# Working the second pair of weight units low part first in the conv stage of a two-layer diffusion trunk

## What is computed

```python
def dwconv3(x, w):
    xp = jnp.pad(x, ((0, 0), (1, 1), (0, 0)))
    return xp[:, :-2] * w[0] + xp[:, 1:-1] * w[1] + xp[:, 2:] * w[2]

def short_conv_mixer(h, w_in, conv_w, w_out):
    y = h @ w_in                      # (256 x 2048) @ (2048 x 6144)
    gb, gc, xv = jnp.split(y, 3, axis=-1)
    return (gb * dwconv3(gc * xv, conv_w)) @ w_out
...
xl = xl + g1 * yl
```

## Time and profile before

| | |
|---|---|
| median of 3 runs | 2545.12 us (2542.32 to 2546.88) |
| the profiled execution | 2542.89 us |
| its span in the trace | 2541.2 us |
| PE, VectorE, ScalarE, GpSimd busy | 98%, 81%, 50%, 8% of the span |
| mean granted TensorE clock | 0.996 |
| input projection, S2 to S23 | 1452 to 1701 us of the span |
| output projection, O0 to O7 | 1701 to 1792 us of the span |

### The profile page before, as it was taken

One profiled execution on the slowest core, in us unless ns is written; L12 is line 12 of the kernel. 1 busy time (PEld: TensorE's weight loads), 2 busy tenths in 40 slices (PEclk: granted clock), 3 DMA queues, 4 the chain that ended last, 5 costly groups with the idle time before them and its releaser, 6 DMA issues.

```text
span 2541.2 us, 38436 instructions
## 1 busy us (share of the span) xinstructions
PE 2499.0 (98%) x13946; PEld 2158.5 (85%) x13946; DVE 2052.4 (81%) x2708; ACT 1265.4 (50%) x1712; POOL 198.6 (8%) x302
## 2 busy tenths in 40 slices
PE   6999999999999999999999999999999999999998
PEld 4778888777988888888888988888988888888886
DVE  6888987897898889987888799989988876764554
ACT  5422334686565555554444544445655555554443
POOL 1002221000000001100111011101000000000000
PEclk9999999999999999999999999999999999999999
DMA  9768987554778778987999699968688756666554
GB/s 355 270 220 267 302 280 232 165 181 148 249 235 270 263 242 277 291 253 235 297 289 299 232 314 349 322 221 276 228 277 270 258 177 196 186 188 203 192 193 147
DMA packets 442817, 625.65 MB, mean 246 GB/s; under 512 B 18693, under 2 KB 359063, under 8 KB 435505
## 3 DMA queue, kind: packets, MB, share of 16 engines
q1 hardware_dynamic: 401888, 450.94, 53.8%
q0 software_dynamic: 40464, 172.59, 21.1%
q10 hardware_dynamic: 320, 0.13, 0.0%
HBM read 621.50 MB, written 2.10 MB: 245 GB/s over the span
## 4 chain that ended last, share of the span: by engine, by line
PE 90%; DVE 5%; DMA 3%; ACT 2%; issue 1%; SPq 0%; DVEq 0%; ACTq 0%
PE ps L2014 46%; PE ps L2022 24%; PE ps L2359 6%; PE ps L2366 3%; PE ps L1934 2%; PE ps L1935 2%; PE ps L1936 2%; DMA raw<-in_sconv_w_in_dram 2%; DVE w_lo L1172 1%; PE ps L2138 1%; PE ps L2156 1%; DVE start_sum L1166 1%; PE ps L2091 1%; PE ps L2090 1%; PE ps L2092 1%
## 5 line engine op out<-in xcount | busy, mean ns | idle before, releaser
L642 ACT ACTIVATE w_hi<-raw 128x1024 fp32r<-128x1024 f32 (+1 forms) x792 | 822.3, 1048 | 913.4 <-PE ps L2022 406.5
L1172 DVE TENSOR_TENSOR w_lo<-raw,w_hi 128x1024 fp32r<-128x1024 f32 (+1 forms) x792 | 954.7, 1210 | 360.6 <-ACT w_hi L642 357.7
L2014 PE MATMUL ps<-xs,w_hi 128*128 128x512 f32 x3200 | 762.3, 393 | 0.5 <-DVE v_rows L1220 0.5
L2014 PEld LDWEIGHTS ps<-xs,w_hi 128*128 128x128 f32 x3200 | 592.2, 188 | 125.3 <-issue 6.7
L2022 PEld LDWEIGHTS ps<-xs,w_lo 128*128 128x128 f32 x3200 | 403.5, 191 | 12.7 <-issue 1.0
L2022 PE MATMUL ps<-xs,w_lo 128*128 128x256 f32 x3200 | 410.0, 283 | 0.7 <-DVE w_lo L1172 0.7
L2359 PE MATMUL ps<-w_hi,act 128*128 128x512 f32 x704 | 175.2, 390 | 0.0
L2014 PE MATMUL ps<-xs_sin,w_hi 128*128 128x512 f32 x704 | 170.0, 392 | 0.4 <-ACT w_hi L642 0.4
L2014 PE MATMUL ps<-act,w_hi 128*128 128x512 f32 x704 | 165.1, 390 | 0.0
L2359 PEld LDWEIGHTS ps<-w_hi,act 128*128 128x128 f32 x704 | 131.6, 188 | 27.1
L540 POOL DMA_DIRECT2D ada_ring<-in_w_ada_dram x128 | 91.0, 711 | 790.8 <-DVE ada_sum L1243 537.2
(11 more groups left out here) (269 smaller groups left out, 2976.3 us busy)
## 6 DMA issues: line engine op xcount, KB each, us to landing
raw<-in_ffn_w_up_dram SPq DMA_DIRECT2D x352, 512.0 KB, 4.7
ada_ring<-in_w_ada_dram POOLq DMA_DIRECT2D x176, 512.0 KB, 5.3
raw<-in_ffn_w_down_dram SPq DMA_DIRECT2D x152, 512.0 KB, 3.7
raw<-in_attn_w_qkv_dram SPq DMA_DIRECT2D x96, 512.0 KB, 4.9
broad_ring<-in_w_ada_dram POOLq DMA_DIRECT2D x48, 1024.0 KB, 6.1
raw<-in_sconv_w_in_dram SPq DMA_DIRECT2D x96, 512.0 KB, 5.6
ada_ring_kv<-in_w_ada_dram POOLq DMA_DIRECT2D x48, 512.0 KB, 5.2
raw<-in_attn_w_o_dram SPq DMA_DIRECT2D x32, 512.0 KB, 4.7
```

The costliest lines, as they stand in the source:

```text
L642: nc.scalar.activation(w_hi[:, slot, 0:n_tiles, :], raw[:, slot, 0:n_tiles, :], ACT.Copy).then_inc(hi_made, 1)
L1172: nc.vector.tensor_tensor(w_lo[:, slot, 0:n_tiles, :], raw[:, slot, 0:n_tiles, :], w_hi[:, slot, 0:n_tiles, :], ALU.subtract).then_inc(lo_ ...
L2014: last = mm(ps[:, bank + m, :], w_hi[:, slot, t, P * m:P * m + P], src[:, tile + t, :], start=(is_first and t == 0), stop=(is_last and t = ...
```

## The change

From i = 1 on, both projections call `mirrored_unit` instead of `paired_unit`: slabs S6 to S23 and O2 to O7, 24 of the 32. Everything else stays as it was.

```diff
@@ narrow
-                        paired_unit(2 * i + (UNITS[phase] // 4 + h), k, 2 * h, src, four_tiles, k, 4)
+                        of_unit = mirrored_unit if phase == "so" and i > 0 else paired_unit
+                        of_unit(2 * i + (UNITS[phase] // 4 + h), k, 2 * h, src, four_tiles, k, 4)
@@ sin_six
-                        paired_unit(6 * i + (UNITS["sin"] // 4 + n), k, 2 * (n % 2), xs_sin, four_tiles, k, 4)
+                        of_unit = mirrored_unit if i > 0 else paired_unit
+                        of_unit(6 * i + (UNITS["sin"] // 4 + n), k, 2 * (n % 2), xs_sin, four_tiles, k, 4)
```

## The result

The changed kernel takes 2546.99 us (median of 20 runs, 2543.11 to 2552.16), the one before 2543.30 (20 runs, 2541.09 to 2547.13). The ratio is 1.0014, 95% interval 1.0007 to 1.0020: 3.7 us slower, 0.14%. In a later comparison of 11 runs with 33 of before it was 1.0019 (1.0010 to 1.0028), 4.5 us. The forecast was +2.7 us, or 2547.8; its base, the median of three runs, was 1.8 us above the 2543.30 of 20.

A forecast was written before the change was run, and what follows sets the result against it. PE was taken as the bound, busy 2499.0 of 2541.2 us, with VectorE and DMA nearly as full. Waits of 4.0 us, less 0.8 and 0.5, gave +2.7 on 2545.12: 2547.8 us, own range 2546.0 to 2549.5.

The forecast's parts named there:

- Term 1: Input and output projections: blocks of 32 matmuls make PE's stream denser, 0.02 us in each of 24 slabs, -0.5 us.
- S6, 2.2 us: Input projection, S6: PE waits 2.1 us for the fourth unit's low copy, plus some 0.1 to get going.
- S7 to S9 covered: Input projection: low copies late by 1.75, 1.64 and 1.13 us cost nothing more, since S6's wait already delays PE.
- rival A: Input projection: low copies come in time, no wait at all, -1.3 us, 2543.8; chance 0.20 together with Rival C.
- S10 to S17, nothing: Input projection: no further wait; S14's lateness of 0.58 us plus 1.3 is covered by PE's 2.2.
- S18, 1.2 to 2.5, taken as 1.8: Input projection, S18: PE waits for a low copy 3.37 us late, less 2.2 of slip, plus 0 to 1.3.
- S19's own wait, -0.8: Input projection, S19: the existing wait for a high copy goes, because PE arrives 4.0 us later; -0.8 us.
- Output projection and transposes, nothing: O2 to O7 have no wait, with cover of only 0.8 us; transposes moved earlier in S22 cost nothing.
- The clock: After a wait of PE: a granted clock below 1.00 would prove the prediction wrong; no cost given.
- Rival B: Input projection: VectorE doesn't stay ahead, all eight waits are paid, 15.2 - 0.5 us, 2559.8; chance 0.07.
- partial form: After S10: two or three of the waits in S14 and S17 to S19 paid again, +5 to +10 us; chance 0.22.
- Rival C: Conv stage, 1500 to 1600: loads are the true bound, PE's order changes nothing, 2544 to 2546; chance 0.20 with rival A.

The follow-up runs named there:

- e3: Changed kernel, but VectorE sums only a quarter of the columns of each broad chunk in the conv stage, loads kept; ratio to the kernel before 1.0000.
- e6: Kernel before the change, with VectorE summing only a quarter of the columns of each broad chunk in the conv stage; ratio to the kernel before 0.9994.
- e14: Changed kernel, but S6 stays paired and the mirrored order begins with S7; ratio to the kernel before 1.0016.
- e5: Changed kernel, but the conv stage's broad chunks load a quarter of their columns while VectorE still sums all; ratio to the kernel before 0.9994.
- e12: The changed kernel itself, timed and profiled anew; ratio to the kernel before 1.0019, median 2547.76 us.
- e11: The changed kernel itself, one more profiled execution; 298.9 us from S6's first matmul to the start of O7's last, no timed ratio.
- e15: Changed kernel, but the input projection is mirrored only from S20 on, the output projection as in the change; ratio to the kernel before 1.0003.
- e10: Kernel before, paired order, but in S6 to S23 PE waits for the fourth unit's low copy before the third's high matmuls; ratio 1.0035.

## Why the prediction was right, point by point

**Term 1, -0.5 us.** Right. Blocks of 32 take 3.83 and 7.28 us, a mirrored slab 11.11 and a paired one 11.13; two executions without waits, e3 and e6, differ by -0.5 to the end of the last matmul.

**S6, 2.2 us.** Right in place and near in size: 2.34, 2.37 and 1.72 us idle in three profiles, foreseen 2.0 to 2.3. To get going again cost 0.3 us and not 0.1, so the term measured 2.6, 2.6 and 2.0. S7 to S9 covered: right, and e14 shows for S7 that it is a cover. But against rival A I wrote that VectorE was late through its own queue without any pause. That looked back only to 1498; the pause that mattered, 2.50 us for a late load, lay in S5. e5 showed it.

**S10 to S17, nothing.** Too low. In the first profile S12 and S13 waited 0.6 and 0.5 us (0.8 each with their restarts). One load of S11 landed 10.0 us after its issue, and VectorE stood still for it just when PE had no slack left (one of S13 took 9.4 us, with a pause of 2.33):

```profile
1561.10 1.23 DVE L1172 TENSOR_TENSOR w_lo<-raw,w_hi 128x1024 fp32r<-128x1024 f32 x1 [2.05 <-ACT w_hi L642]
```

I took the landings of one execution as given. They differ from one execution to the next, and this is the term that was missing: each late load may turn into a wait. The other two profiles of the changed kernel have 0.3 and 0.4 us in S12 and nothing in S13.

**S18, 1.2 to 2.5, taken as 1.8.** Right in size: 1.25, 1.24 and 1.24 idle in the changed kernel's three profiles, and the slab 1.5 to 1.7 us longer. The working behind it fits one of them. I took 3.37 us of lateness, less a slip of PE of 2.2, plus 0 to 1.3 by which VectorE's stream would come later. Counted from S6's start, e12 has a slip of 2.2 ahead of S18 and a fourth copy 0.3 later than before, as foreseen. e11 has 4.4 and 2.4, the first profile 5.6 and 3.6: there two errors cancel. Slip beyond the first 2 us thus bought nothing at S18, since the copy moved with PE. The likely route is the one that I named for S10 to S16, ScalarE waiting for PE to give slots back; no run tests it alone. **S19's own wait, -0.8:** gone, as foreseen. **Output projection and transposes, nothing:** right.

**The clock.** I named it only as something that would prove me wrong, and put no cost on it. In two of three profiles it added 1.6 us.

**The sum.** +2.7 foreseen; +3.7 and +4.5 in the two comparisons. From S6 to S23 I foresaw +2.8; the three profiles have 6.2, 4.9 and 2.9. The first profiled execution, 2548.09 us, was foreseen at 2545.6 and lies 5.2 us above before, beyond the +4.4 of my upper end. Waits in S12 and S13 and the clock, each 1.6 us, cost the most that I had put at nothing. That the median 2546.99 lies 0.8 us from my 2547.8 is in part luck, because a base that was 1.8 us too high made up for a difference that was 1.0 too low. **Rival B**, eight waits of 15.2 us in all, did not come: four waits of 4.7 us. Its partial form, waits that come back after S10, came in a small way in S12 and S13. **Rival C**, the bytes as the bound, falls with e3, where the same demand let PE run without a wait. The limit of about 358 GB/s that I cited from the Trainium skill ("DMA: Bandwidth & Descriptors", "Specifications") is no ceiling here: the trace shows 388 GB/s over 4 us after S6's wait, and 376 over the 20 us from 1504.

No version that leaves nothing out beats the kernel before: the order's own gain is 0.5 us at most, and the best use of it (e15) can't be told from before.

## What to carry to other kernels

An order of work that gains 0.02 us a slab can move a deadline by 3.66 us. So look up, for the engine that feeds the bound one, by how much each of its results is early, and do that where it is fullest. Late results need not be added up: as long as the late engine does not wait for the one that is held up, the first wait covers those behind it, as S6's did for S7 to S9. A late load starts the count anew, and so does any place where the late engine's work has moved with the bound one: S18's wait was 1.24 us after PE had slipped by 2.2 us and 1.25 after 5.6. And look at the idle time of the feeding engine well ahead of the first late result, since VectorE at 95% load carried a pause of 2.5 us through a whole slab.

## What was not expected of the hardware

In S6, after PE had stood still for 2.34 and 2.37 us, the granted clock fell to 0.5 (1.2 GHz) for 3.4 us; after 4.78 us (e10) it stayed there for 6.8. After 1.72 (e12), 1.97 (e14) and 1.25 us of idle in this stage it stayed at 1.00. The length of the idle time does not decide alone, though: early in e3's trace, where PE has more gaps, the clock fell at 49.2 after an idle of 1.96 us that ended at 48.4. In the changed kernel the fall came 0.9 and 0.8 us after PE had begun to work again, so the 32 high matmuls behind the wait paid for it, 1.5 and 1.4 us, and not the wait itself. In e10 it came at 1507.8, 0.6 us before PE began again at 1508.41.
